# Delta rule: the second head's transposed inverse moves to the other partition half, and the inversion products of both heads use all four quarters of the array

## The reference

```python
kk = einsum('bnhrd,bnhsd->bnhrs', k, k)
a_low = where(strict, beta[..., None] * kk * decay_mat, 0.0)
sol = triangular_solve(a_low + eye, rhs, left_side=True, lower=True, unit_diagonal=True)
u, w = sol[..., :dv], sol[..., dv:]
def step(state, xs):
    q_c, k_c, qk_c, u_c, w_c, gl_c = xs
    v_new = u_c - w_c @ state
    o = q_c @ state + qk_c @ v_new
    state = state * gl_c + k_c.T @ v_new
    return state, o
```

## Time and profile before

| | us |
|---|---|
| median of 3 runs | 2885.29 (2885.14 to 2887.12) |
| the profiled execution | 2885.75 |
| its span in the trace | 2883.9 |
| TensorE busy in the span | 2832.7 (98%) |
| VectorE busy | 1456.6 (51%) |
| ScalarE busy | 1081.3 (37%) |

### The profile page before, as it was taken

The page is one execution under the profiler, slowest core; times in us unless marked ns, Lnnn a source line. Parts: engine busy times, 40 slices in busy tenths (PEclk is TensorE's granted clock), DMA queues, the critical chain, the costliest instruction groups (busy, mean ns, idle before and its releaser), DMA issues.

```text
span 2883.9 us, 43564 instructions
## 1 busy us (share of the span) xinstructions
PE 2832.7 (98%) x19606; PEld 2337.1 (81%) x19606; DVE 1456.6 (51%) x1431; ACT 1081.3 (37%) x1176; POOL 146.1 (5%) x74
## 2 busy tenths in 40 slices
PE   9999999999999999999999999999999998999998
PEld 7788778888888888888888888788877886888886
DVE  6676553443455544443364444466657665543432
ACT  5554542222454832222342222442235532332222
POOL 1000010000110010000110000240000000100001
PEclk9999999999999999999999999999999999999999
DMA  4220022223222022233222223322231003222232
GB/s 150 74 77 2 31 88 102 97 93 110 103 100 88 35 73 94 97 102 110 102 88 102 95 95 115 104 83 81 88 125 35 4 6 135 101 96 97 102 102 74
DMA packets 44953, 249.09 MB, mean 86 GB/s; under 512 B 8507, under 2 KB 12347, under 8 KB 17248
## 3 DMA queue, kind: packets, MB, share of 16 engines
q1 hardware_dynamic: 43616, 242.11, 24.6%
q10 hardware_dynamic: 1152, 4.19, 0.4%
HBM read 237.90 MB, written 8.39 MB: 85 GB/s over the span
## 4 chain that ended last, share of the span: by engine, by line
PE 91%; DVE 5%; ACT 3%; issue 1%; DMA 0%; SPq 0%; DVEq 0%; ACTq 0%
PE ps L667 76%; PE ps L2919 4%; PE ps L1515 1%; PE ps L2501 1%; PE ps L2211 1%; PE ps L3979 1%; PE ps L2926 1%; PE ps L2485 1%; PE ps L3962 1%; PE ps L3991 1%; PE ps L2182 0%; DVE wlo L274 0%; PE ps L3097 0%; DVE gdn_conv L1147 0%; ACT whi L268 0%
## 5 line engine op out<-in xcount | busy, mean ns | idle before, releaser
L274 DVE TENSOR_TENSOR wlo<-wraw,whi 128x2048 fp32r<-128x2048 f32 x210 | 486.6, 2317 | 911.5 <-ACT whi L268 907.3
L268 ACT ACTIVATE whi<-wraw 128x2048 fp32r<-128x2048 f32 x210 | 402.1, 1915 | 900.0 <-PE ps L667 900.0
L667 PE MATMUL ps<-ffn_xh,whi 128*128 128x512 f32 x1408 | 549.2, 390 | 0.2 <-DVE wlo L274 0.2
L667 PE MATMUL ps<-ffn_xh,wlo 128*128 128x512 f32 x1408 | 547.8, 389 | 0.0
L667 PE MATMUL ps<-ffn_xl,whi 128*128 128x512 f32 x1408 | 547.8, 389 | 0.0
L667 PEld LDWEIGHTS ps<-ffn_xh,whi 128*128 128x128 f32 x1408 | 264.3, 188 | 56.9 <-DVE wlo L274 1.0
L667 PEld LDWEIGHTS ps<-ffn_xl,whi 128*128 128x128 f32 x1408 | 264.3, 188 | 55.6 <-issue 0.7
L667 PEld LDWEIGHTS ps<-ffn_xh,wlo 128*128 128x128 f32 x1408 | 264.3, 188 | 54.9
L667 PE MATMUL ps<-ffn_uh,whi 128*128 128x512 f32 x704 | 274.1, 389 | 0.0
L667 PE MATMUL ps<-ffn_uh,wlo 128*128 128x512 f32 x704 | 273.9, 389 | 0.0
L667 PE MATMUL ps<-ffn_ul,whi 128*128 128x512 f32 x704 | 273.9, 389 | 0.0
(11 more groups left out here) (524 smaller groups left out, 4446.5 us busy)
## 6 DMA issues: line engine op xcount, KB each, us to landing
wraw<-in_weights SPq DMA_DIRECT2D x211, 1024.0 KB, 4.8
gates_kept<-gates_tmp ACTq DMA_DIRECT2D x8, 512.0 KB, 4.0
mix_gate<-gates_kept SPq DMA_DIRECT2D x8, 512.0 KB, 11.0
h<-in_x SPq DMA_DIRECT2D x4, 512.0 KB, 9.0
mix_y<-hz_kept SPq DMA_DIRECT2D x2, 1024.0 KB, 6.3
out<-out SPq DMA_DIRECT2D x4, 512.0 KB, 3.1
wraw<-in_weights SPq DMA_DIRECT2D x2, 512.0 KB, 7.4
ple_raw<-in_p SPq DMA_DIRECT2D x4, 256.0 KB, 5.1
```

Of the source, the lines that this page charges most:

```text
L268: c.nc.scalar.activation(c.whi[:, j % 2, :], c.wraw[:, j % 2, :], ACT.Copy).then_inc(c.hi_ready, 1)
L274: c.nc.vector.tensor_tensor(c.wlo[:, j % 2, :], c.wraw[:, j % 2, :], c.whi[:, j % 2, :].bitcast(F32), ALU.subtract).then_inc(c.lo_ready, 1)
L667: last = nc.tensor.matmul(pair[:, m, :], a, b, start=opens and n == 0 and wa + xa == 0, stop=closes and n == len(ks) - 1 and wa == 1)
```

## The change

The first head stays as it was. The second head's XT (`XX[:, 1, 1]`) now lies in the opposite partition half from its X: what belongs to the low half is in partitions 64 to 127, and the other way round. So a product of the second head goes across (`across`): from low rows to high output partitions and from high rows to low. `pe_left` and `pe_right` issue, chunk by chunk, a `both` of head 0 and an `across` of head 1, four products in four quarters. The outputs lie in two banks, 3 and 4, one for each head. Since bank 3 is also a bank of qk, `pe_left` of level 0 now waits for both `attT`; before, `pe_right` of level 0 had that wait. On VectorE the subtract of s = 2 and each transpose become three instructions (`homes`): head 0 with all partitions, and two of 64 partitions that read one half and write the other. Y21 and X12 issue the two heads in two different quarters in turn, X12 with its second output in the MISC bank; ScalarE's two copies after the last level become four, and the one after X12 becomes two.

```diff
+    def across(self, out, a, b):
+        for rows, other in zip(self.halves(), reversed(self.halves())):
+            last = self.c.nc.tensor.matmul(out(other), a(rows), b(rows), start=True, stop=True)
+        return last
...
+    def items(self, first, width):
+        both = self.c.ps[:, self.Y_BANK - 1:self.Y_BANK + 1, :].rearrange("p h (n t) -> p (h n) t", t=P)
+        return both[:, :, first:first + width]
+    def lefts(self):
+        return self.items(0, HALF)
+    def rights(self):
+        return self.items(HALF, HALF // 2)
...
@@ pe_build, Y21 and X12
-            for h in range(2):
-                for n in range(NC):
-                    last = nc.tensor.matmul(Y[high, h * NC + n, :], self.Aoff[:, h, n, :], self.XX[low, 0, h, n, :],
+            for n in range(NC):
+                for h, to in enumerate((high, low)):
+                    last = nc.tensor.matmul(Y[to, n, :], self.Aoff[:, h, n, :], self.XX[low, 0, h, n, :],
...
+            second = self.chunks(self.misc(pe, self.at("X12c", k)), HALF)
...
@@ pe_left
             pe.wait_ge(*self.at("AT", 3 * k + 1))
+            pe.wait_ge(*self.at("attT", 2 * k + 1))
...
-        for h in range(2):
-            for n in range(NC):
-                last = self.both(...)
+        for n in range(NC):
+            for h, products in enumerate((self.both, self.across)):
+                last = products(...)
@@ act_build
-            nc.scalar.activation(self.XTf[low, :, :, 0:HALF], self.XX[low, 1, :, :, :], ACT.Copy)
-            nc.scalar.activation(self.XTf[high, :, :, HALF:], self.XX[high, 1, :, :, :], ACT.Copy)\
-                .then_inc(*self.done("Xd"))
+            for h, (first, second) in enumerate(((low, high), (high, low))):
+                nc.scalar.activation(self.XTf[low, h, :, 0:HALF], self.XX[first, 1, h, :, :], ACT.Copy)
+                last = nc.scalar.activation(self.XTf[high, h, :, HALF:], self.XX[second, 1, h, :, :], ACT.Copy)
...
@@ dve_build and dve_right
-            nc.vector.transpose(self.both_sides(0), self.both_sides(1)).then_inc(*self.done("X0"))
+            for h, to, rows in self.homes():
+                last = nc.vector.transpose(self.head(0, h)[rows, :], self.head(1, h)[to, :])
+            last.then_inc(*self.done("X0"))
...
+    def homes(self):
+        low, high = self.halves()
+        return (0, slice(0, P), slice(0, P)), (1, low, high), (1, high, low)
...
-            nc.vector.transpose(self.both_sides(1), self.both_sides(0)).then_inc(*self.done("XX"))
+            for h, to, rows in self.homes():
+                last = nc.vector.transpose(self.head(1, h)[to, :], self.head(0, h)[rows, :])
+            last.then_inc(*self.done("XX"))
```

More of the change, by code:

```diff
@@ L1598, in pe_build @@
         elif s == 27:
+            low, high = self.halves()
+            second = self.chunks(self.misc(pe, self.at("X12c", k)), HALF)
             pe.wait_ge(*self.at("Y21c", k))
-            low, high = self.halves()
-            for h in range(2):
-                for n in range(NC):
-                    last = nc.tensor.matmul(Y[low, h * NC + n, :], self.Y[high, h, n, :], self.XX[high, 1, h, n, :],
+            for n in range(NC):
+                for h, (rows, out) in enumerate(((high, Y[low, NC + n, :]), (low, second[low, n, :]))):
+                    last = nc.tensor.matmul(out, self.joined()[rows, n, :], self.XX[rows, 1, h, n, :],
                                             start=True, stop=True)
@@ L1637, in pe_left @@
             pe.wait_ge(*self.at("AT", 3 * k + 1))
+            pe.wait_ge(*self.at("attT", 2 * k + 1))
             if k:
                 pe.wait_ge(*self.at("X12c", k - 1))
-        for h in range(2):
-            for n in range(NC):
-                last = self.both(lambda r: Y[r, h * NC + n, :], lambda r: self.Ac[r, h, n, :], lambda r: self.XX[r, 0, h, n, :])
+        Y = self.lefts()
+        for n in range(NC):
+            for h, products in enumerate((self.both, self.across)):
+                last = products(lambda r: Y[r, h * NC + n, :], lambda r: self.Ac[r, h, n, :], lambda r: self.XX[r, 0, h, n, :])
         last.then_inc(*self.done("Y"))
@@ L1646, in pe_right @@
         i = LV * k + l
-        X, XT = (self.halved(self.Z_BANK + b) for b in range(2))
         pe.wait_ge(*self.at("Yc", i))
-        if l == 0:
-            pe.wait_ge(*self.at("attT", 2 * k + 1))
-        else:
+        if l:
             pe.wait_ge(*self.at("XX", i - 1))
[L1653 to L1656, removed]
+        X, XT, Y = self.rights(), self.turned(), self.compact()
+        for n in range(NC):
+            for h, products in enumerate((self.both, self.across)):
+                last = products(lambda r: X[r, h * NC + n, :], lambda r: self.XX[r, 1, h, n, :],
+                                lambda r: Y[r, h * NC + n, :])
         last.then_inc(*self.done("Z"))
@@ L1660, in pe_right @@
                 for n in range(NC):
-                    last = self.both(lambda r: XT[r.start:r.start + HALF // 2, h * NC + n, :],
-                                     lambda r: self.Y[r, h, n, 0:HALF // 2], lambda r: self.XX[r, 1, h, n, HALF // 2:])
+                    last = self.both(lambda r: XT[r.start:r.start + HALF // 2, n, h, :],
+                                     lambda r: Y[r, h * NC + n, :], lambda r: self.XX[r, 1, h, n, HALF // 2:])
             last.then_inc(*self.done("ZT"))
@@ L1732, in act_build @@
             act.wait_ge(*self.at("Y21", k))
[L1733 removed]
+            nc.scalar.activation(self.joined().rearrange("p n t -> p (n t)"), Y[:, 0:T // 2], ACT.Copy)\
                 .then_inc(*self.done("Y21c"))
@@ L1898, in dve_off, with head @@
             .then_inc(*self.done("AT"))
-    def both_sides(self, x):
-        return self.XX[:, x, :, :, :].rearrange("p h n t -> p (h n t)")
+    def homes(self):
+        low, high = self.halves()
+        return (0, slice(0, P), slice(0, P)), (1, low, high), (1, high, low)
+    def head(self, x, h):
+        return self.XX[:, x, h, :, :].rearrange("p n t -> p (n t)")
     def dve_right(self, dve, k, l):
         nc, i, half = self.c.nc, LV * k + l, HALF // 2
-        X, XT = (self.XX[:, x, :, :, :].rearrange("p h n t -> p (h n) t") for x in range(2))
+        X = self.XX[:, 0, :, :, :].rearrange("p h n t -> p (h n) t")
         dve.wait_ge(*self.at("Z", i))
```

37 lines of the change are left out of this document (23 added, 14 removed).

## The result

| | before | the change |
|---|---|---|
| median (6 runs each) | 2885.74 (2885.14 to 2890.05) | 2898.78 (2896.69 to 2902.83) |
| ratio | | 1.0044, 95% interval 1.0031 to 1.0057 |
| profiled execution, its span | 2885.75, 2883.9 | 2897.62, 2895.8 |
| first "AT" to the last "vn" product of the stage | 143.96 | 157.57 |

The change is 13 us slower; 2889.6 was forecast, and 2898.78 lies above the range. The last line of the table is how the stage is measured from here on: from VectorE's first "AT" to the start of the last `vn` product that reads `gdn_R` (207.64 to 351.60 before, 206.58 to 364.15 after). It grows by 13.61 us, where the two profiled executions differ by 11.9 in all, so nothing of the loss lies outside it.

A forecast was written before the change was run, and what follows sets the result against it. TensorE was taken as the bound, with thin cover over VectorE's chain. Three builds at +1.24 us (3.7) and +0.6 for the first gave +4.3 on 2885.29: 2889.6 us, range 2880 to 2898.

The forecast's parts named there:

- Quarters: TensorE's products in four quarters instead of two: 0.47 us saved per pe_left or pe_right call; X12 and Y21 save 0.49.
- Pieces: VectorE's subtract and transposes as three instructions each: 1.44 us per transpose until the next instruction, 1.38 per subtract.
- The dearer crossing: Rival: VectorE instructions crossing partition halves cost more, up to 0.52 us a set, +8.3, 2898 us; chance 0.15.
- The second build: Second pair, one "AT" to the next: +2.15, -0.94, +0.32, +0.31, +0.80 and -1.4, together +1.24 us.
- the last part: Second pair, level 3 to the next "AT": shorter products against ScalarE's extra copies and a later state copy, -1.4 us.
- The first build: First pair: pe_left 0 some 2.0 us later, then -0.94, +0.3, +0.3, +0.8 and about -1.9, leaving +0.6 us.
- a tail of about -1.9: End of the first pair's build: about 1.9 us shorter, since without steps ahead nothing delays it.
- the clock: TensorE's longer idle times could lower its granted clock from 1.00; nothing counted, as idle time is in short pieces.
- quarters that don't run together: Rival: four quarters go no faster than two, products cost as now, about +13 us, 2898 us; chance 0.05.

The follow-up runs named there:

- kernel before with straight pieces: Kernel before, every subtract and transpose of the four builds split into three instructions, none crossing partition halves, products in two quarters: 2903.31 us, ratio 1.0060.
- the run with fillers: The change plus fp32 products that nobody reads in TensorE's idle times of the first pair's build and at the end of the last: 2894.34 us, 1.0028 to before.
- The kernel with two quarters at a time: The change with pe_left and pe_right ordered head by head, eight products of both, then eight of across: 2902.05 us, ratio 1.0057 to before.
- the kernel with pieces in the first build: Kernel before, only the first pair's subtract and first transpose split into three instructions each, none crossing partition halves: 2887.75 us, ratio 1.0007.

## Why the prediction was wrong

**Quarters: right.** The eight steps of four rows lie 0.061 us apart (the first `both` at 251.27, the eighth at 251.70), where the later stage's rows gave 0.062, and a call takes 0.63 to the next line instead of 1.08. Y21 and X12 take 0.68 instead of 1.14. The Trainium skill (TensorE: Matmul & The Clock Gate, Part 3: Packing small matmuls) lets a weight load overlap with running products only where its row group differs. This case's trace doesn't agree: `both` and `across` share their two row groups, and four row starts fit in 0.061, two for each group, where one quarter alone had one in that time (X12 in the earlier trace rows).

Putting the calls back to two quarters costs about 1 us in each of the two stretches at full clock, and 4 in the stage as it ran: little of the 18.8 us by which they had been relieved (the other 3.9 are Y21 and X12, which that run leaves as they are) reaches the end.

**Pieces: right in size.** 1.38 for three transposes with the way to the next instruction (1.44 forecast), 1.33 for the subtracts (1.38). The dearer crossing did not come. In the kernel before with straight pieces the three take 1.22: there the first two start in the same partition, and the sum of three at 0.45 would be 1.35, so they overlap; where each starts in another half the three take that 1.35. By the Trainium skill (VectorE: DVE Perf Modes, section Two Vector instructions with no wait between them) an instruction is held until the earlier ones have finished where it starts in another quadrant than the one before. Both numbers agree.

**The second build: right in its steps, short by 0.67.** Forecast 7.20 from "AT" to `pe_left` 0, then 2.18, 5.20, 4.64, 5.44 and 8.86; measured 7.56, 2.23, 5.23, 4.64, 5.25 and 9.28, together +1.91 for +1.24. Two parts were mis-sized. The first product comes 0.26 after the end of `attT`, for which I had taken 0.05, and VectorE's copy of the state ahead of the mask starts 0.21 later after "AT" than before (2.25 for 2.04), which I had booked in the last part. And that part, from level 3 to the next "AT", with ScalarE's extra copies, gained 0.98 and not 1.4.

**The first build, by the run with fillers: the same term again.** Against the kernel before, `pe_left` 0 comes 1.91 later (forecast 2.0), the way to the first `copy_predicated` is 0.87 shorter (0.94), the levels are 0.34, 0.35 and 0.73 longer (0.3, 0.3, 0.8), and the rest 1.07 shorter where I had "a tail of about -1.9". That makes +1.39 for +0.6. Over four builds the waits cost 6.86 where the sum was 4.3; in the two builds taken apart here the tail is 0.83 and 0.42 of the 0.79 and 0.67 that the sum was short by. What in it holds the gain back no run took apart; in the waits above, the preparation's chain through MISC (`gdn_eg`, 3.3 us against 0.5 before) and X12 waiting for ScalarE's copy (1.6 against 0.8) have grown.

**The step that failed is the clock.** "I count nothing for that, since the idle time is in short pieces": it was worth 5.08 us in the first build and 1.73 at the end of the stage, 6.75 of 13.61. The pieces of idle time are short (the longest 2.29), and it fell. Falls came behind a single idle time of 1.72 to 2.30 us, and behind levels in which TensorE was busy for 2.3 to 3.0 of 4 us; neither always brought one.

**The rivals.** The two at 2898, dearer crossing pieces and quarters that don't run together, gave the right time for a wrong reason. The chance of a slower result should have had a case of its own for the clock, since the change's very aim is a less busy TensorE in a stage that it no longer bounds.

**Open.** Why the first build and the end of the stage lose the clock and the builds between do not is not settled by any run. The change's second build has stretches as sparse as those ahead of the falls, and the clock stays:

```profile
249.00:253.00 4.00, 1.77 (x54) 1.53 (x54) 3.06 (x7) 0.51 (x2) 0.00 (x0) 1.00 0.00 0
253.00:257.00 4.00, 2.97 (x75) 2.31 (x67) 3.45 (x9) 0.64 (x2) 0.00 (x0) 1.00 0.01 4
```

The recurrence of the pair before runs between its levels, with products that fill the array; whether that is the reason wasn't tried. The kernel with two quarters at a time, with 2.30 us of idle time and full clock behind it, says that something besides the length of an idle time decides. The 6.75 us are what the stages of two profiled executions differ by; the medians differ by 4.44, and the clock outside the stage differs from execution to execution as well. Why it does wasn't looked into.

## What to carry to other kernels

Relief for the busiest engine is worth what the next engine's queue lets through: count first, in the two timelines, what the other engine must do in each round, and don't pay for the relief with its time. Moving the exchange to two engines with time to spare, with fillers and the wait reordered, turned +13 us into -6. Where a change thins out TensorE's work, price the stretch at half clock as a case of its own, and where it happens try products that nobody reads in the idle times: here 18 of them gave back 2 us of stage in one kernel, 35 gave 6.75 in another.

## What the hardware showed that I had not expected

- The granted clock fell to half behind stretches with TensorE busy for 2.86 and 2.96 of 4 us, and held at 1.00 through 3.18 and 3.38 in the kernel before; elsewhere it held through 1.77. The busy share alone does not tell when it falls. Once down, it stayed there for some 20 us of sparse work, and came back within some 4 us where dense work followed (0.50 in the kernel with pieces in the first build from about 214.7 to 217.7).
- Filling the one long idle time did not save the clock: of the two falls of the first build (at about 212.6 and 219.5) it took away the first, and the second came at about 224.
- Stages that no edit touched differ in clock between executions: 0.98 over 2400 to 2500 us in the profiled ones of the kernel before and of the change, 0.95 in that of the kernel with fillers in the first build. Its six executions had mean clocks of 0.995 to 0.999 and took 2899.06 to 2891.37.
- A copy of 64x256 across the partition halves takes 0.40 us on GpSimd, 0.42 on ScalarE; now and then one on GpSimd took 1.24 to 1.29.
